# Second attention of a two-block transformer kernel: order of score matmuls, gate steps and ScalarE copies

## The chip, the cores and the metric

The program runs on one core of a Trainium2 chip. The metric is the time on the device in microseconds (us), from one launch that computes everything from the inputs in HBM to the output. TensorE (PE) multiplies, VectorE (DVE), ScalarE (ACT) and GpSimd (POOL) work on what it leaves in PSUM, and SyncE issues most loads. Each engine runs its own list of instructions in order and waits on semaphores.

## The reference

Two transformer blocks follow each other over 512 tokens of width 1024. The change is in the second one's attention. There, after an RMS norm, one wide projection `h @ w_in` gives, besides others, q, k, v (3 groups of 4 heads, head size 64) and the logits of two gates:

```
for g, (window, dil) in enumerate(((128, 1), (512, 4), (2048, 16))):
    o, lse = banded_window_attention(q_g, k_g, v_g, window // dil)   # over tokens of one residue mod dil
alpha = softmax(stack(lses))            # over the three groups
y_b = sum_g alpha_g * o_g
gates = sigmoid(gate_logits)
merged = gates[0] * (y_a @ w_branch_a) + gates[1] * (y_b @ w_branch_b)
x = x + merged @ w_out
```

The weights of the mixture over the groups make it one softmax over the keys of all three groups, and so the kernel computes it: for a head place the scores of the three groups lie side by side and get one maximum, one sum and one sum of values.

## The kernel before

Matmuls of float32 data are made of three products of rounded high and low parts. So each slab of weights (1 MB, 8 pieces of 128 rows by 256 columns) is loaded by SyncE into a ring of four buffers, its high part is copied by ScalarE (`hi`) and its low part is computed by VectorE (`lo`, or `lo_half` for half a slab) into one of the split buffers `wsq0` and `wsq1`, which the slabs use in turn. Tensor `steps(...)` is a generator: it issues six matmuls of 512 columns (two pieces of 128 rows, three products), then yields.

The second attention is done in two stages, jj = 0 and 1, one for each pair of the four head places. A stage goes so:

1. For each group g of 0, 1, 2, the slab `("qk", jj, g)` is multiplied, 8 steps: q first (m = 0), then k (m = 1), each for both heads of the pair. The result is rotated: VectorE shuffles rows and multiplies by the cosines (into `tb` for q and `X` for k), GpSimd multiplies the shuffled rows by the sines and adds, ScalarE makes the high parts (`rope_hi`, signal `a_rope`), VectorE the low parts (`rope_lo`, signal `v_rope`, tile `k2l` for k).
2. Some steps of the gate's projection. Its four slabs `("g1", n)` have 8 steps each, 32 in all, and are one generator `more` (`beside2`) that goes on through both stages, 16 steps in the first and 15 in the second; the last one comes after the loop. Every engine has its own `more`, in which each step holds what that engine has to do for it: on ScalarE step 4 of each half slab is the sigmoid of the gate, and the first step of a slab is the `hi` copy of the next slab; on VectorE step 4 is the multiplication by `row` that empties the PSUM bank, with the low parts of the next slab in steps 3 and 4 of the slab.
3. For each residue r of 0 to 3 (tokens r, r+4, ...): `scores2(jj, r)` issues the 18 score matmuls (two heads; for each of the three groups high, low and mask) into PSUM banks 2 to 4. It waits first for the rotation of group 2, and by `hold` for the exponentials of the residue before, which read the same banks. `soft2` is the maximum (VectorE) and the exponential (ScalarE), `normalise2` the division (VectorE), `turn2` the 12 transposes on TensorE (three lots of four through banks 6, 7, 6) and their three copies to `pT` on ScalarE, `values2` the product with v on TensorE, its high part on ScalarE and its low part on VectorE. Transposes follow the scores by one residue, values by two. The last two residues of stage 0 are finished inside the qk slabs of stage 1.

After the second stage `m_back` reloads a spilled tile (`M2b<-m_spill`) on ScalarE's queue; the sums of both branches and the product with `w_out` need it. The order on each engine is written out by hand in three parallel loops, one each in `tensor`, `scalar` and `vector`, and these are what the change edits. In a trace all matmuls bear line 492 and all transposes line 495, all activations line 1250, all VectorE tensor-tensor operations line 1896.

Of the kernel before, what the change touches and what calls it, by code (L numbers as in the profile page):

```python
# [8 lines left out]
P = 128  # L9
T = 512  # L10
# [21 lines left out]
M2_0, M2_1, M2_2 = 0, 516, 644  # L32
# [73 lines left out]
def emit(nc, a, out, top):  # L106
# [11 lines left out]
    S = {}  # L118
# [12 lines left out]
    ps = top.enter_context(nc.psum_tensor("ps", [P, 8 * 512], F32))  # L131
# [170 lines left out]
    mk2 = at("mk2", M_END2, BF16, sq + 31232)  # L302
    idb2 = at("idb2", 128, BF16, sq + 31624)
# [4 lines left out]
    q2v = q2[:, :].rearrange("p (g i t) -> p g i t", g=3, i=2)  # L308
    k2hv = k2h[:, :].rearrange("p (g i t) -> p g i t", g=3, i=2)
    k2lv = k2l[:, :].rearrange("p (g i t) -> p g i t", g=3, i=2)  # L310
# [162 lines left out]
        return 0 if 2 * (k + 1) <= s.nk else 1  # L473

    early_units, units = 8, 4 * 7 + 8 * 12

    def paced(it, place):

# [6 lines left out]
    def tensor(engine):  # L485
        pe = Engine(engine)
# [4 lines left out]
        def mm(o, l, r, start, stop):  # L491
            return pe.e.matmul(o, l, r, start=start, stop=stop, skip_group_check=True)  # L492
# [4 lines left out]
        def hold(b, frees):  # L497

            for signal, key in free[b]:
                pe.wait_ge(S[signal], key)  # L500
            free[b] = frees
# [285 lines left out]
        more = beside()  # L787
# [4 lines left out]
        for it in range(32):  # L792
            g, n = it // 8, it % 8
# [37 lines left out]
        for k in range(8):  # L831
            i = mm(ps[0:16, 5 * 512:5 * 512 + 1], wrv[:, k, :], sh2[:, k:k + 1], k == 0, k == 7)
# [7 lines left out]
        for r in range(2):  # L840
            for half in range(2):
                i = mm(ps[64 * half:64 * half + 64, 6 * 512 + 128 + 8 * r:6 * 512 + 136 + 8 * r], ident[:, r:P:2],
                       both[:, half:16:2], True, True)
# [48 lines left out]
        for i in range(4):  # L892
            t = tr(ps[0:16, 6 * 512 + i * P:6 * 512 + (i + 1) * P], af[:, i * 16:(i + 1) * 16], ident)
# [191 lines left out]
        turn["banks"] = [0, 1]  # L1085
        free["scores"] = free[2] + free[3] + free[4]

        def scores2(jj, r):
            for i in range(2):
                s0, s1 = (4 * 512, 3 * 512 + 256) if i else (2 * 512, 3 * 512)  # L1090
                S0 = ps[:, s0:s0 + 512]
                qa = q2v[:, 0, i, r:T:4]
                pe.wait_ge(S["a_rope"], (jj, 2, 1))
                pe.wait_ge(S["v_rope"], (jj, 2, 1))
                if i == 0:
                    hold("scores", [("a_soft", (jj, r, 1, 2))])
                mm(S0, qa, k2hv[:, 0, i, :], True, False)
                mm(S0, qa, k2lv[:, 0, i, :], False, False)
                pe.wait_ge(S["mask2_in"], "mask2")
                pe.wait_ge(S["v_set"], "idb2")  # L1100
                mm(S0, idb2[:, :], mk2[:, M2_0 + 3 - r:M2_0 + 515 - r], False, True)
                for g in (1, 2):
                    S1 = ps[:, s1 + (g - 1) * P:s1 + g * P]
                    qa = q2v[:, g, i, r:T:4]
                    mm(S1, qa, k2hv[:, g, i, r:T:4], True, False)
                    mm(S1, qa, k2lv[:, g, i, r:T:4], False, False)
                    mo = M2_1 if g == 1 else M2_2
                    t = mm(S1, idb2[:, :], mk2[:, mo:mo + P], False, True)
                t.then_inc(*S["pe_score"].tick((jj, r, i, 2)))

        def turn2(jj, r):
            for c0 in (0, 2, 4):
# [25 lines left out]
        more = beside2()  # L1138
        scored = turned = None
        for jj in range(2):  # L1140
            for g in range(3):
                pieces = steps([("qk", jj, g)], H2h, H2l, T, lambda m: [("v_rope", (jj, g, m, "cos"))])
                for _ in range(4):
                    next(pieces)
                if turned and g < 2:
                    values2(*turned)
                    turned = scored
                    scored = None
                    if turned:
                        turn2(*turned)  # L1150
                for _ in pieces:
                    pass
            for _ in range(4):
                next(more)
            for r in range(4):
                scores2(jj, r)
                next(more, None)
                next(more, None)
                if turned:
                    values2(*turned)  # L1160
                if r < 3 or jj == 0:
                    next(more, None)
                turned = scored
                scored = (jj, r)
                if turned:
                    turn2(*turned)
# [70 lines left out]
    def scalar(engine):  # L1237
# [521 lines left out]
        def turn2(jj, r):  # L1759
            for c0 in (0, 2, 4):  # L1760
                ac_.wait_ge(S["pe_turn"], (jj, r, c0, 2))
                if jj or r:
                    k = 4 * jj + r - 1
                    ac_.wait_ge(S["pe_value"], (k // 4, k % 4, 2))
                act(pT2[:, c0 * 256:c0 * 256 + 512], bank(6 + (c0 // 2) % 2), ACT.Copy).then_inc(
                    *S["a_turn"].tick((jj, r, c0, 2)))
# [11 lines left out]
        for jj in range(2):  # L1778
            for g in range(3):
                pieces = fill2(("qk", jj, g))  # L1780
                for _ in range(4):
                    next(pieces)
                if turned and g < 2:
                    values2(*turned)
                    turned = scored
                    scored = None
                    if turned:
                        turn2(*turned)
                for _ in pieces:
                    pass  # L1790
            for _ in range(4):
                next(more)
            for r in range(4):
                soft2(jj, r)
                next(more, None)
                next(more, None)
                if turned:
                    values2(*turned)
                if r < 3 or jj == 0:
                    next(more, None)  # L1800
                turned = scored
                scored = (jj, r)
                if turned:
                    turn2(*turned)
        for _ in more:
            pass
        hi(slabs["bb"])
# [82 lines left out]
    def vector(engine):  # L1890
# [783 lines left out]
        for jj in range(2):  # L2674
            for g in range(3):
                pieces = fill2(("qk", jj, g))
                for _ in range(4):
                    next(pieces)
                if turned and g < 2:
                    values2(*turned)  # L2680
                    turned = scored
                    scored = None
                for _ in pieces:
                    pass
            for _ in range(4):
                next(more)
            for r in range(4):
                soft2(jj, r)
                next(more, None)
                next(more, None)  # L2690
                normalise2(jj, r)
                if turned:
                    values2(*turned)
                if r < 3 or jj == 0:
                    next(more, None)
                turned = scored
                scored = (jj, r)
        for _ in more:
# [285 lines left out]
```

## Time and profile before

| what | value |
|---|---|
| median of 3 runs | 1957.14 us (1951.63 to 1957.41) |
| profiled execution, its own time | 1954.66 us |
| its span, first to last instruction | 1952.8 us |
| mean granted TensorE clock | 0.975 |
| PE busy | 1844.9 us, 94% of the span |
| DVE busy | 983.0 us, 50% |
| ACT busy | 654.9 us, 34% |
| POOL busy | 85.1 us, 4% |
| chain that ended last | PE 80%, DVE 9%, DMA 4%, ACT 4%, issue 2%, POOL 1% |

The span lies 1.9 us under the time of its own execution. A granted clock of 1.00 is 2.4 GHz and 0.50 is 1.2 GHz; a stretch in between is a mixture. The busy share of 94% counts matmuls that run at the lower clock in full, so it hides their slowness as well as short waits. The second attention lies between 1320 and 1516 us of the span.

### The profile page before, as it was taken

The numbers are of one execution on the slowest core, as the hardware profiler recorded it, in microseconds if no ns is written. First come the engines' busy times: TensorE is split into PE (matmuls) and PEld (weight loads), VectorE is DVE, ScalarE is ACT, GpSimd is POOL, SyncE is SP. The second block draws the span as 40 slices with busy tenths as digits, with TensorE's granted clock in tenths as the row PEclk, the third lists the DMA queues.
The fourth block names the chain that finished last, engine by engine and source line by source line (L and its number), as shares of the span: only waits on it lengthen the run. The fifth ranks groups of instructions, "written<-read, shape, count | busy, mean of one in ns | idle before, by whom it ended". The sixth has DMA issues, their size and how long they took to land.

```text
span 1952.8 us, 22760 instructions
## 1 busy us (share of the span) xinstructions
PE 1844.9 (94%) x9397; PEld 1336.6 (68%) x9403; DVE 983.0 (50%) x1620; ACT 654.9 (34%) x1126; POOL 85.1 (4%) x70
## 2 busy tenths in 40 slices
PE   5999999999999699999999899998998899999998
PEld 4877887788878434343443278897777788888886
DVE  4887887833542322231322153638384556536643
ACT  4455554432232301020110053424555333213233
POOL 0200001000000000000000000003030200000000
PEclk9999999999999699999999999999999999999999
DMA  9342423452351499999999942272121422233221
GB/s 323 127 130 77 141 76 98 130 173 87 103 231 68 167 415 421 421 422 421 420 421 422 409 141 81 70 220 65 44 84 38 156 71 85 89 119 105 73 89 43
DMA packets 174521, 355.10 MB, mean 182 GB/s; under 512 B 7154, under 2 KB 144466, under 8 KB 149074
## 3 DMA queue, kind: packets, MB, share of 16 engines
q1 hardware_dynamic: 170672, 338.85, 47.1%
q10 hardware_dynamic: 3458, 14.50, 2.1%
q8 instruction: 74, 1.21, 0.3%
q0 software_dynamic: 288, 0.30, 0.1%
q14 instruction: 29, 0.24, 0.0%
HBM read 345.53 MB, written 8.39 MB: 181 GB/s over the span
## 4 chain that ended last, share of the span: by engine, by line
PE 80%; DVE 9%; DMA 4%; ACT 4%; issue 2%; POOL 1%; SPq 0%; ACTq 0%; DVEq 0%
PE ps L492 77%; PE ps L495 3%; DMA rx<-in_w_exp_down 1%; DMA rx<-in_w_exp_up 1%; POOL X L2813 1%; DMA md<-in_w_mod 1%; DVE wsq1l L1896 1%; DVE wsp0l L1896 1%; DVE X L1905 1%; DVE small L2141 1%; ACT M L1250 1%; DVE k2l L1896 0%; ACT KR L1250 0%; DMA M2b<-m_spill 0%; DVE tb L1896 0%
## 5 line engine op out<-in xcount | busy, mean ns | idle before, releaser
L492 PE MATMUL ps<-H,wsq1h 128*128 128x512 f32 x640 | 200.4, 394 | 4.7 <-DVE wsq1l L1896 2.7
L492 PE MATMUL ps<-H,wsq0h 128*128 128x512 f32 x608 | 191.2, 396 | 0.2 <-DVE wsq0l L1896 0.2
L492 PE MATMUL ps<-rx,XE 128*64 128x512 f32 x752 | 178.5, 606 | 2.8 <-DMA rx<-in_w_exp_up 2.2
L492 PE MATMUL ps<-H,wsp1h 128*128 128x512 f32 x544 | 172.6, 399 | 1.4 <-DVE wsp1l L1896 1.4
L492 PEld LDWEIGHTS ps<-H,wsq1h 128*128 128x128 f32 x640 | 120.2, 190 | 30.6 <-issue 6.0
L492 PEld LDWEIGHTS ps<-H,wsq0h 128*128 128x128 f32 x608 | 114.5, 190 | 25.6 <-issue 2.3
L492 PE MATMUL ps<-H,wsq1l 128*128 128x512 f32 x320 | 125.3, 391 | 0.0
L492 PE MATMUL ps<-H,wsp0h 128*128 128x512 f32 x368 | 121.4, 408 | 2.1 <-ACT H L1250 2.1
L1896 DVE TENSOR_TENSOR wsq1l<-ring,wsq1h 128x1024 fp32r<-128x1024 f32 (+2 forms) x72 | 82.8, 1190 | 77.9 <-ACT wsq1h L1250 77.9
L492 PE MATMUL ps<-H,wsq0l 128*128 128x512 f32 x304 | 119.1, 392 | 0.0
L492 PEld LDWEIGHTS ps<-rx,XE 128*64 128x64 f32 x752 | 49.7, 138 | 95.9 <-issue 84.8
L492 PEld LDWEIGHTS ps<-H,wsp1h 128*128 128x128 f32 x544 | 99.8, 190 | 22.0 <-issue 3.5
L492 PE MATMUL ps<-H,wsp1l 128*128 128x512 f32 x272 | 106.8, 393 | 0.0
L1905 DVE SCALAR_TENSOR_TENSOR X<-ps,modT,X 128x512 f32<-128x512 f32 x72 | 53.8, 749 | 100.0 <-PE ps L492 100.0
L1896 DVE TENSOR_TENSOR wsq0l<-ring,wsq0h 128x1024 fp32r<-128x1024 f32 (+3 forms) x72 | 80.5, 1159 | 43.7 <-ACT wsq0h L1250 43.2
L492 PE MATMUL ps<-rx,hT 128*64 128x512 f32 x368 | 96.0, 604 | 1.5 <-DMA rx<-in_w_exp_down 1.4
L1250 ACT ACTIVATE tb<-ps 128x512 f32<-128x512 f32 (+1 forms) x44 | 26.1, 592 | 190.1 <-PE ps L492 190.1
L1250 ACT ACTIVATE wsq1h<-ring 128x1024 fp32r<-128x1024 f32 (+2 forms) x72 | 66.0, 964 | 56.0 <-PE ps L492 48.7
L492 PE MATMUL ps<-KR,wsp0h 128*128 128x512 f32 x256 | 78.8, 389 | 0.0
L1250 ACT ACTIVATE wsq0h<-ring 128x1024 fp32r<-128x1024 f32 (+3 forms) x72 | 64.2, 940 | 42.6 <-PE ps L492 40.3
L492 PEld LDWEIGHTS ps<-H,wsp0h 128*128 128x128 f32 x368 | 65.8, 192 | 16.7 <-issue 3.6
L492 PE MATMUL ps<-H,wsp0l 128*128 128x512 f32 x184 | 72.8, 396 | 0.0
(378 smaller groups left out, 3458.6 us busy)
## 6 DMA issues: line engine op xcount, KB each, us to landing
rx<-in_w_exp_gate SPq DMA_DIRECT2D x49, 1024.0 KB, 17.2
rx<-in_w_exp_down SPq DMA_DIRECT2D x46, 1024.0 KB, 20.7
rx<-in_w_exp_up SPq DMA_DIRECT2D x45, 1024.0 KB, 19.1
ring<-in_w_in SPq DMA_DIRECT2D x37, 1024.0 KB, 5.5
ring<-in_w_up SPq DMA_DIRECT2D x20, 1024.0 KB, 5.2
ring<-in_w_exp_up SPq DMA_DIRECT2D x19, 1024.0 KB, 20.5
ring<-in_w_mod SPq DMA_DIRECT2D x18, 1024.0 KB, 7.3
ring<-in_w_exp_down SPq DMA_DIRECT2D x18, 1024.0 KB, 19.0
```

The lines of the kernel that those rows point to most:

```text
L492: return pe.e.matmul(o, l, r, start=start, stop=stop, skip_group_check=True)
L495: return pe.e.transpose(o, i, idn)
L1250: return ac_.e.activation(o, i, f, **kw)
L1896: return v.e.tensor_tensor(o, x, y, op)
L1905: return v.e.scalar_tensor_tensor(o, x, s, y, op0, op1)
L2141: v.e.reduce_max(small[:, k:k + 1], ps[:, lo:lo + W + 256], axis=AX.X).then_inc(*S["v_soft"].tick((g, n, "max", i)))
L2813: return g_.e.tensor_tensor(o, x, y, op)
```

## The change

Four edits. On TensorE `scores2` gets a list of groups and waits for each group's rotation just ahead of its matmuls. The scores of groups 0 and 1 of residue 0 are issued right after the last qk slab, ahead of the gate's steps; those of group 2 follow after them. Six gate steps instead of four come ahead of group 2 (or of `soft2` on the other engines). The steps of the residues are 3, 3, 2, 2 in stage 0 and 3, 3, 2, 1 in stage 1 instead of 3, 3, 3, 3 and 3, 3, 3, 2. ScalarE takes the steps of a residue last, behind `values2` and `turn2`, where before two came ahead of `values2` and the third ahead of `turn2`.

```
--- before.py
+++ after.py
@@ -474,6 +474,11 @@
 
     early_units, units = 8, 4 * 7 + 8 * 12
 
+    def paced2(jj, r):
+
+        return {(0, 0): (2, 1), (0, 1): (2, 1), (0, 2): (1, 1), (0, 3): (1, 1),
+                (1, 0): (2, 1), (1, 1): (2, 1), (1, 2): (1, 1), (1, 3): (1, 0)}[jj, r]
+
     def paced(it, place):
 
         upto = lambda k: (units - early_units) * k // 128
@@ -1085,28 +1090,31 @@
         turn["banks"] = [0, 1]
         free["scores"] = free[2] + free[3] + free[4]
 
-        def scores2(jj, r):
+        def scores2(jj, r, groups=(0, 1, 2)):
+
             for i in range(2):
                 s0, s1 = (4 * 512, 3 * 512 + 256) if i else (2 * 512, 3 * 512)
-                S0 = ps[:, s0:s0 + 512]
-                qa = q2v[:, 0, i, r:T:4]
-                pe.wait_ge(S["a_rope"], (jj, 2, 1))
-                pe.wait_ge(S["v_rope"], (jj, 2, 1))
-                if i == 0:
-                    hold("scores", [("a_soft", (jj, r, 1, 2))])
-                mm(S0, qa, k2hv[:, 0, i, :], True, False)
-                mm(S0, qa, k2lv[:, 0, i, :], False, False)
-                pe.wait_ge(S["mask2_in"], "mask2")
-                pe.wait_ge(S["v_set"], "idb2")
-                mm(S0, idb2[:, :], mk2[:, M2_0 + 3 - r:M2_0 + 515 - r], False, True)
-                for g in (1, 2):
-                    S1 = ps[:, s1 + (g - 1) * P:s1 + g * P]
+                for g in groups:
+                    pe.wait_ge(S["a_rope"], (jj, g, 1))
+                    pe.wait_ge(S["v_rope"], (jj, g, 1))
+                    pe.wait_ge(S["mask2_in"], "mask2")
+                    pe.wait_ge(S["v_set"], "idb2")
                     qa = q2v[:, g, i, r:T:4]
-                    mm(S1, qa, k2hv[:, g, i, r:T:4], True, False)
-                    mm(S1, qa, k2lv[:, g, i, r:T:4], False, False)
-                    mo = M2_1 if g == 1 else M2_2
-                    t = mm(S1, idb2[:, :], mk2[:, mo:mo + P], False, True)
-                t.then_inc(*S["pe_score"].tick((jj, r, i, 2)))
+                    if g == 0:
+                        S0 = ps[:, s0:s0 + 512]
+                        if i == 0:
+                            hold("scores", [("a_soft", (jj, r, 1, 2))])
+                        mm(S0, qa, k2hv[:, 0, i, :], True, False)
+                        mm(S0, qa, k2lv[:, 0, i, :], False, False)
+                        mm(S0, idb2[:, :], mk2[:, M2_0 + 3 - r:M2_0 + 515 - r], False, True)
+                    else:
+                        S1 = ps[:, s1 + (g - 1) * P:s1 + g * P]
+                        mm(S1, qa, k2hv[:, g, i, r:T:4], True, False)
+                        mm(S1, qa, k2lv[:, g, i, r:T:4], False, False)
+                        mo = M2_1 if g == 1 else M2_2
+                        t = mm(S1, idb2[:, :], mk2[:, mo:mo + P], False, True)
+                if groups[-1] == 2:
+                    t.then_inc(*S["pe_score"].tick((jj, r, i, 2)))
 
         def turn2(jj, r):
             for c0 in (0, 2, 4):
@@ -1150,16 +1158,18 @@
                         turn2(*turned)
                 for _ in pieces:
                     pass
-            for _ in range(4):
+
+            scores2(jj, 0, (0, 1))
+            for _ in range(6):
                 next(more)
             for r in range(4):
-                scores2(jj, r)
-                next(more, None)
-                next(more, None)
+                scores2(jj, r, (0, 1, 2) if r else (2,))
+                for _ in range(paced2(jj, r)[0]):
+                    next(more)
                 if turned:
                     values2(*turned)
-                if r < 3 or jj == 0:
-                    next(more, None)
+                for _ in range(paced2(jj, r)[1]):
+                    next(more)
                 turned = scored
                 scored = (jj, r)
                 if turned:
@@ -1788,20 +1798,18 @@
                         turn2(*turned)
                 for _ in pieces:
                     pass
-            for _ in range(4):
+            for _ in range(6):
                 next(more)
             for r in range(4):
                 soft2(jj, r)
-                next(more, None)
-                next(more, None)
                 if turned:
                     values2(*turned)
-                if r < 3 or jj == 0:
-                    next(more, None)
                 turned = scored
                 scored = (jj, r)
                 if turned:
                     turn2(*turned)
+                for _ in range(sum(paced2(jj, r))):
+                    next(more)
         for _ in more:
             pass
         hi(slabs["bb"])
@@ -2682,17 +2690,17 @@
                     scored = None
                 for _ in pieces:
                     pass
-            for _ in range(4):
+            for _ in range(6):
                 next(more)
             for r in range(4):
                 soft2(jj, r)
-                next(more, None)
-                next(more, None)
+                for _ in range(paced2(jj, r)[0]):
+                    next(more)
                 normalise2(jj, r)
                 if turned:
                     values2(*turned)
-                if r < 3 or jj == 0:
-                    next(more, None)
+                for _ in range(paced2(jj, r)[1]):
+                    next(more)
                 turned = scored
                 scored = (jj, r)
         for _ in more:
```

## Rows read from the trace of the kernel before

**Rows 1.** What TensorE waited for from 1325 to 1530 us: total, times, longest.

```profile
PE ps L495 <- ACT pT L1250: 8.6, 8, 3.1
PE ps L492 <- ACT k2h L1250: 7.4, 2, 3.7
PE ps L492 <- DVE X L1896: 5.9, 1, 5.9
PE ps L492 <- DVE ybl L1896: 2.1, 1, 2.1
PE ps L492 <- DVE wsq1l L1896: 1.5, 1, 1.5
```

**Rows 2.** TensorE in stretches: length, busy (matmuls), granted clock, DMA share, GB/s.

```profile
1352.97:1410.69 57.72, 48.04 (x251) 0.91 0.19 55
1448.73:1508.77 60.04, 52.25 (x287) 0.89 0.17 53
1354.60:1360.40 5.80, 5.68 (x24) 1.00 0.42 120
1364.06:1368.36 4.30, 4.30 (x17) 0.67 0.16 30
1368.36:1372.81 4.45, 4.45 (x20) 0.93 0.60 210
1372.81:1376.28 3.47, 3.47 (x20) 1.00 0.00 0
1376.28:1380.49 4.21, 4.21 (x20) 1.00 0.00 0
1385.08:1389.40 4.32, 4.32 (x20) 0.61 0.00 0
1389.40:1393.94 4.54, 4.54 (x15) 0.62 0.00 0
1393.94:1398.59 4.65, 4.40 (x43) 1.00 0.71 220
1398.59:1402.26 3.67, 3.67 (x20) 1.00 0.03 11
1458.35:1463.25 4.90, 4.90 (x18) 0.50 0.31 82
1503.81:1508.77 4.96, 4.71 (x46) 1.00 0.00 0
```

**Rows 3.** TensorE in order of time: start, us, and in brackets the idle time before.

```profile
1373.89 0.44 PE L492 MATMUL ps<-k2h,q 128*128 128x128 f32 x1
...
1374.45 0.58 PE L492 MATMUL ps<-k2h,q 128*128 128x512 f32 x1
...
1410.28 0.66 PE L495 MATMUL ps<-cst,pp 128*128 128x128 f32 x4 [1.06 <-ACT pT L1250]
```

**Rows 4.** VectorE in order of time, around the first residue.

```profile
1361.17 2.79 DVE L1896 TENSOR_TENSOR k2l<-X,tbr 64x512 fp32r<-64x512 f32 x4
1363.99 2.36 DVE L1896 TENSOR_TENSOR wsq0l<-ring,wsq0h 128x1024 fp32r<-128x1024 f32 x2
1366.27 0.68 DVE L1896 TENSOR_TENSOR X<-ps,tb 128x512 f32<-128x512 f32 x1
1368.64 1.82 DVE L2643 TENSOR_REDUCE small<-ps 128x1 f32<-128x768 f32 x2 [1.69 <-PE ps L492]
```

**Rows 5.** ScalarE in order of time, exponentials of residues 0 and 1, copies behind.

```profile
1372.24 0.20 ACT L1250 ACTIVATION_READ_ACCUMULATOR pp<-ps,small 128x1 f32 x1
...
1380.31 1.28 ACT L1250 ACT_TABLE_LOAD   x1
1381.61 0.63 ACT L1250 ACTIVATE X<-X 128x512 f32<-128x512 f32 x1
1382.14 1.99 ACT L1250 ACTIVATE wsq1h<-ring 128x1024 fp32r<-128x1024 f32 x2
1384.03 1.06 ACT L1250 ACTIVATE pT<-ps 128x512 f32<-128x512 f32 x2
```

**Rows 6.** The chain of work that ended last, at the end of the second stage.

```profile
1510.35 8.02 DMA M2b<-m_spill
```

## The prediction

> **What bounds the kernel now.** The clock of the core comes first: a mean of 0.975 (in the table above), so somewhere TensorE ran below its full rate. The page's chain of work that ended last is mostly TensorE, so a microsecond counts where TensorE stands or runs slow. The change touches the second attention alone, so the next view is what TensorE waited for there [rows 1]. The reader should see four causes that the edits could touch: ScalarE's copies of transposes (8.6 us in 8 waits, longest 3.1), the rotation of group 2 (7.4 us in 2 waits of 3.7), the low part of a slab (1.5 us), and, untouched, 5.9 us for the sums behind the reload. Then the windows [rows 2]: the stage proper, from the end of the last qk slab to the end of the last transposes inside it, takes 57.72 us in the first stage. In the second, with the last gate step, a value product and one more lot of transposes, it takes 60.04. Their clocks are 0.91 and 0.89, where the stretches in them without a long wait have 1.00.
>
> The clock is the second half of the loss. The scores of one residue take 3.47 us at clock 1.00, but 4.30 at 0.67 behind the 3.7 us wait, 4.90 at 0.50 in the second stage, and 4.32 at 0.61 behind the 3.1 us wait; the two gate steps behind the latter take 4.54 at 0.62 [rows 1, 2]. Three steps at full clock take 4.21, so two take 2.81, and 1.7 us is lost there alone. Behind the 1.5 us wait the clock stayed at 1.00 [rows 1, 2]. So each wait of over 3 us costs its length and some 1.2 to 2.7 us more. A gate step is 4.21/3 = 1.40 us (three at clock 0.93 took 4.45).
>
> **The change part by part.** It removes and adds no arithmetic: the same matmuls, the same 31 steps in the loops, no DMA issue in a queue that another work would pass. What changes is when TensorE stands. I walk it.
>
> *Start of stage 0.* From 1352.97 the two first groups' scores can run: the rotation of group 1 lies one slab, some 11 us, back. Of the 3.47 us of scores, the third group's share is 2 x (1374.45 - 1373.89) = 1.12 us [rows 3], so the first two are 2.35. Behind them TensorE is at 1355.3, and the slab's low part, which it had waited for until about 1354.6, is there. Six steps at 1.40 take 8.4 us: 1363.7. The low part of k for group 2 ends at 1361.17 + 2.79 = 1363.96 [rows 4], and scores began at 1364.06 [rows 2]. This chain (VectorE, GpSimd, ScalarE, VectorE) doesn't depend on scores and stays. So both waits, 1.5 and 3.7, shrink to some 0.4 us, the clock has no reason to fall, and at 1364.06 only 1.12 us of scores are left where before 4.30 were: TensorE has them at 1365.2.
>
> *First residue's exponentials: a new wait.* VectorE makes the next slab's low parts at 1363.99 (2.36) and empties the gate's bank at 1366.27 (0.68), so it is free at 1366.95 [rows 4]: it is now late for the maximum, where before it waited for TensorE until 1368.64. From there to the end of the second exponential's sum were 1372.24 + 0.20 - 1368.64 = 3.80 us [rows 4, 5], so they end at 1370.8. TensorE has done three steps at 1365.2 + 4.2 = 1369.4 and must hold the next scores until 1370.9. The new wait is 1.5 us, as long as the one after which the clock held.
>
> *Rest of stage 0.* Residue 1: scores 3.47, three steps 4.21. Its transposes cost 1.70 us when the copies keep pace: 4.65 (values, a step, transposes) less a step of 1.4 and values of 1.5, with the usual wait of about 0.25 in them. Before they waited 3.1, as ScalarE had a table load (1.28), a sigmoid and a slab's high part (1.99) in front of the first copy at 1384.03 [rows 5]. Now that work lies between the exponentials of residues 0 and 1. From 1370.8 it is 1.28 + 0.63 + 1.99 + 1.28 (table back) = 5.2, so ScalarE is ready at 1376.0; the maximum of residue 1 is ready at 1370.9 + 3.47 + 2.15 = 1376.5. It just fits, by 0.5 us. Residues 2 and 3: scores 3.67, one step 1.4, then 4.65, which is 9.7 each [rows 2]; the 1.06 us wait of residue 3 [rows 3] shrinks to 0.25, since the sigmoid is no longer ahead of the copy. Sum: (1370.9 - 1352.97) + 3.47 + 4.21 + 1.70 + 2 x 9.7 = 46.7 us against 57.72. **11.0 us saved.**
>
> *Stage 1.* The same chain runs 94.3 us later (scores at 1458.35 for 1364.06 [rows 2]), but its last slab ended at 1448.73, which is 95.8 later: TensorE has 1.5 us less to fill. 2.35 + 8.4 brings it to 1459.5, behind the rotation: no wait. Third group and three steps, 1.12 + 4.2: 1464.8; the exponentials end at 1370.8 + 94.3 = 1465.1, a hold of 0.3. Then 3.47 + 4.21 + 1.70, residue 2 9.7. Residue 3 has only one step: scores 3.67, step 1.4, values 1.5, transposes at +6.6. The exponentials of the same residue end about 4.0 us behind the scores, then ScalarE copies the values' high part (0.4) before it takes the first transposes' copy, done at 3.67 + 4.9 = 8.6 where TensorE wants it at 7.8. Transposes thus cost 2.5: a new wait of 0.8. Sum: 16.4 + 9.4 + 9.7 + 9.1, and the tail of 4.96 as before [rows 2], is 49.6 against 60.04. **10.4 us saved.**
>
> *The tail.* The reload M2b (8.02 us [rows 6]) is issued by ScalarE behind the last copies, so it and the 5.9 us wait behind it [rows 1] move forward with them and neither grows. The qk slabs of stage 1 keep their length: their high parts are made by ScalarE one slab ahead. With the sigmoid now behind the copies, the first of these ends some 2 us later against TensorE, still 2 us before VectorE wants it.
>
> **Sum:** 11.0 + 10.4 = 21.4 us. Against the profiled execution's own time, 1954.66 - 21.4 = 1933.3. The median of the runs shown lies 2.5 us above that execution, and one run 3.0 below, so I say **1934**. If each new wait (0.4, 1.5, 0.3, 0.8) cost nothing it would be 3.0 us less, 1930, and with the spread of the runs 1927; if the holds reach 3 us, see the second case.
>
> **A rule to weigh.** The table loads on ScalarE stand in the trace with 1.28 us, and the sigmoid begins 0.02 us behind the load [rows 5]. The Trainium skill (ScalarE: Activation LUTs, What ACT_TABLE_LOAD costs) gives about 2.66 us for a switch, of which about 1.38 is a drain. By that the two switches between the exponentials of residues 0 and 1 would take 2.8 us more; the trace shows no such drain here. This bears on the third case below.
>
> **The rivals.**
> 1. *As walked* (0.70): 1934, own range 1928 to 1939.
> 2. *The hold lets the clock fall* (0.12). The scores of residue 1 must wait for residue 0's exponentials, behind VectorE's low parts. If that hold is 3 us instead of 1.5 and 0.3, it costs 1.5 and 2.7 us more and a lowered clock of 2.5 us, in both stages: 21.4 - 9.2 = 12.2 saved, 1942 by the profiled time. For it: the hold is real. Against: it needs 1.5 us that no row has.
> 3. *ScalarE becomes late for residue 1* (0.08). The margin is 0.5 us. With 2.8 us more there, the exponentials start 2.3 late and the copies, which had 0.4 us of slack, cost TensorE 1.9 us in each stage: 17.6 saved, 1937. This is what the skill's figure (ScalarE: Activation LUTs) would bring about; the rows show 1.28.
> 4. *The stage gets shorter and the end doesn't* (0.07): something behind, such as the reload or a load of `w_out`, is bound to another time, and TensorE's 5.9 us wait grows by most of the gain: 1945 to 1955. Against it: the reload's place in ScalarE's order, and a DMA share of 0.17 to 0.19 in the stages [rows 2].
> 5. *Slower* (0.03): TensorE, with more short holds of 0.25 to 1.5 us in a row, is granted the lower clock for most of both stages. Scores at 0.50 took 4.90 for 3.47, that is 1.41 times; 90 us of such work would cost 37 us more, 16 over what is saved: 1970. It decides from 21.4/0.41 = 52 us at the lower clock. Against: the stretch with value products and transposes, with its short wait, has 1.00 [rows 2].
>
> **Chances.** What differs by under 0.3% (5.9 us) can't be told from no change by a measurement of this kernel. Faster 0.92 (cases 1 to 3 and part of 4), same 0.05 (the rest of 4), slower 0.03. The range of 1927 to 1943 holds cases 1, 2 and 3.
>
> **What the profile of the changed kernel would show.** The window from the end of the last qk slab to the last transposes of the stage near 46.7 and 49.6 us, at clock 0.98 or more. The waits for the rotation under 1 us in all. Waits for `pT` of about 0.25 each, and one near 1.1 in the last residue of stage 1. A new wait of TensorE's score matmuls for ScalarE's exponentials, 1.5 and 0.3 us. The reload some 21 us earlier, its 8 us and the 5.9 us behind it unchanged. The prediction is wrong if the score matmuls of residue 0 or 2 still take over 4 us, if the hold passes 3 us, or if the 5.9 us wait grows.

## The result and the profile after

The changed kernel takes 1929.72 us (median of 4 runs, 1927.24 to 1932.09) against 1954.59 us (4 runs, 1951.63 to 1957.41): a ratio of 0.9878, 95% interval 0.9860 to 0.9897, or 20 to 27 us. The profiled execution took 1927.24 us, its span 1925.4. Line 492 is line 497 here, 495 is 500, 1250 is 1260, 1896 is 1904.

The windows of the changed kernel, TensorE alone (length, busy, matmuls, granted clock, DMA share, GB/s):

```profile
0.00:1346.27 1346.27, 1275.29 (x6745) 0.98 0.60 227
1346.27:1502.03 155.76, 143.35 (x809) 0.99 0.22 75
1502.03:1925.40 423.37, 413.74 (x1842) 0.99 0.28 90
1346.27:1393.58 47.31, 44.93 (x249) 1.00 0.22 67
1393.58:1431.50 37.92, 37.67 (x208) 1.00 0.16 56
1431.50:1481.38 49.88, 47.84 (x286) 1.00 0.19 64
1481.38:1502.03 20.65, 12.90 (x73) 0.91 0.43 153
1364.19:1367.87 3.68, 3.68 (x17) 1.00 0.02 6
```

The same cuts of the kernel before, as far as [rows 2] don't have them:

```profile
0.00:1352.97 1352.97, 1280.27 (x6745) 0.98 0.60 226
1352.97:1529.58 176.61, 150.98 (x811) 0.92 0.20 66
1529.58:1952.80 423.22, 413.67 (x1842) 0.99 0.28 90
1410.69:1448.73 38.04, 37.79 (x207) 1.00 0.16 56
1508.77:1529.58 20.81, 12.90 (x73) 0.91 0.42 152
```

The reader should see three things. First, everything the change touches lies in the second line of each: from the end of the last qk slab of stage 0 to the product with `w_out`, 176.61 us became 155.76: **20.85 us**. I call this the stretch. Second, inside it the two stages [rows 2] went from 57.72 to 47.31 and from 60.04 to 49.88, at clock 1.00 in place of 0.91 and 0.89; the qk slabs between them and the part behind them stayed to 0.2 us. TensorE's busy time in the stretch fell from 150.98 to 143.35: so 7.6 of the 20.85 us are matmuls that had run at the lower clock, and the other 13.2 are waits. Third, the two profiled executions differ by 27.4 us, and 6.7 of that lies ahead of the stretch, in code that is the same. I take that for spread between executions: over the 14 profiles of this study, all with the same code up to there, the stretch begins anywhere from 1345.01 to 1356.38 us, while what follows it lasts 423.2 to 424.5, and 23 timed runs of the kernel before lie between 1947.59 and 1958.42. So the stretch, and not a profile's whole time, prices an edit here, and 20.85 lies inside the interval of the timed runs.

What TensorE waited for in it (1325 to 1520 us):

```profile
PE ps L497 <- DVE X L1904: 5.7, 1, 5.7
PE ps L500 <- ACT pT L1260: 2.4, 8, 0.7
PE ps L497 <- DVE ybl L1904: 2.1, 1, 2.1
PE ps L497 <- ACT pp L1260: 1.9, 2, 1.2
PE ps L497 <- DVE k2l L1904: 0.4, 1, 0.4
```

L497 are the matmuls, L500 the transposes; `pT` stands for ScalarE's copies, `pp` for its exponentials, `k2l` for the rotation. Against [rows 1], the copies' 8.6 us became 2.4, the rotation's 7.4 and the slab's 1.5 became 0.4, and 1.9 us for the exponentials are new. The wait behind the reload stayed. In order of time the first two look so:

```profile
1357.44 0.46 PE L497 MATMUL ps<-k2h,q 128*128 128x128 f32 x1 [0.38 <-DVE k2l L1904]
1364.19 0.62 PE L497 MATMUL ps<-k2h,q 128*128 128x512 f32 x1 [1.25 <-ACT pp L1260]
```

And ScalarE between the exponentials of residues 0 and 1, where [rows 5] had the transposes' copies queued behind sigmoid and slab:

```profile
1363.94 0.20 ACT L1260 ACTIVATION_READ_ACCUMULATOR pp<-ps,small 128x1 f32 x1
1364.15 1.28 ACT L1260 ACT_TABLE_LOAD   x1
1365.45 0.63 ACT L1260 ACTIVATE X<-X 128x512 f32<-128x512 f32 x1
1365.98 1.99 ACT L1260 ACTIVATE wsq1h<-ring 128x1024 fp32r<-128x1024 f32 x2
1367.99 1.28 ACT L1260 ACT_TABLE_LOAD   x1
1370.02 0.90 ACT L1260 ACTIVATE pp<-ps,small 128x768 f32<-128x768 f32 x1 [0.74 <-DVE small L1910]
```

The slack of 0.5 us that was forecast is 0.74.

### The profile page after: what moved, and what is told of

The parts are those of the page before. It is cut to its first block, busy times and chain, and to the rows that moved or that the text cites. A ratio compares the mean times of both kernels' runs of the same rounds, so it can differ in the third digit from the quotient of the medians.

```text
span 1925.4 us, 22762 instructions
## 1 busy us (share of the span) xinstructions
PE 1832.4 (95%) x9395; PEld 1329.9 (69%) x9403; DVE 983.1 (51%) x1620; ACT 654.6 (34%) x1126; POOL 85.3 (4%) x70
## 4 chain that ended last, share of the span: by engine, by line
PE 80%; DVE 9%; DMA 4%; ACT 3%; issue 2%; POOL 1%; SPq 0%; ACTq 0%; DVEq 0%
PE ps L497 77%; PE ps L500 3%; DMA rx<-in_w_exp_down 1%; DMA rx<-in_w_exp_gate 1%; POOL X L2821 1%; DVE wsq1l L1904 1%; DMA md<-in_w_mod 1%; DVE k2l L1904 1%; DVE wsp0l L1904 1%; DVE X L1913 1%; DVE small L2149 1%; DVE wsq0l L1904 1%; ACT M L1260 1%; ACT KR L1260 0%; DVE tb L1904 0%
## 5 line engine op out<-in xcount | busy, mean ns | idle before, releaser
L497 PE MATMUL ps<-H,wsq1h 128*128 128x512 f32 x640 | 198.6, 392 | 3.2 <-DVE H L1913 2.0
L497 PE MATMUL ps<-H,wsq0h 128*128 128x512 f32 x608 | 189.2, 393 | 0.0
L497 PE MATMUL ps<-rx,XE 128*64 128x512 f32 x752 | 176.6, 600 | 2.8 <-DMA rx<-in_w_exp_up 2.2
L497 PE MATMUL ps<-H,wsp1h 128*128 128x512 f32 x544 | 172.8, 399 | 1.4 <-DVE wsp1l L1904 1.4
L497 PEld LDWEIGHTS ps<-H,wsq1h 128*128 128x128 f32 x640 | 119.1, 188 | 28.3 <-issue 4.1
L497 PEld LDWEIGHTS ps<-H,wsq0h 128*128 128x128 f32 x608 | 113.4, 188 | 24.5 <-issue 1.7
L497 PE MATMUL ps<-H,wsq1l 128*128 128x512 f32 x320 | 124.7, 390 | 0.0
L497 PE MATMUL ps<-H,wsp0h 128*128 128x512 f32 x368 | 119.6, 403 | 2.1 <-ACT H L1260 2.1
L497 PE MATMUL ps<-H,wsq0l 128*128 128x512 f32 x304 | 118.5, 390 | 0.0
L497 PEld LDWEIGHTS ps<-H,wsp1h 128*128 128x128 f32 x544 | 99.9, 190 | 21.9 <-issue 3.5
L497 PEld LDWEIGHTS ps<-rx,XE 128*64 128x64 f32 x752 | 49.3, 136 | 94.3 <-issue 83.2
L497 PE MATMUL ps<-H,wsp1l 128*128 128x512 f32 x272 | 106.9, 393 | 0.0
L497 PE MATMUL ps<-rx,hT 128*64 128x512 f32 x368 | 96.6, 604 | 1.4 <-DMA rx<-in_w_exp_down 1.3
L497 PE MATMUL ps<-KR,wsp0h 128*128 128x512 f32 x256 | 78.8, 389 | 0.0
L497 PEld LDWEIGHTS ps<-H,wsp0h 128*128 128x128 f32 x368 | 64.5, 188 | 16.4 <-issue 3.6
L1260 ACT ACTIVATE Yh<-ps,small 128x512 fp32r<-128x512 f32 x16 | 10.1, 684 | 184.4 <-PE ps L497 184.4
```

Of the source, the lines that this page charges most:

```text
L1260: return ac_.e.activation(o, i, f, **kw)
```

## The experiments

Stretch lengths are read as above, from a window that begins where the last qk slab of stage 0 ends and goes to the first matmul with `w_out`. All ratios are against the kernel before.

| kernel | stretch, us | less than 176.61 by | ratio, 95% interval |
|---|---|---|---|
| changed kernel | 155.76 | 20.85 | 0.9878 (0.9860 to 0.9897) |
| scores alone (e1) | 172.28 | 4.33 | 0.9973 (0.9957 to 0.9989) |
| steps alone (e2, e11) | 164.87, 164.52 | 11.74, 12.09 | 0.9946 (0.9927 to 0.9965) |
| copies first alone (e3) | 166.31 | 10.30 | 0.9954 (0.9936 to 0.9971) |
| waits filled (e4) | 169.74 | 6.87 | 0.9956 (0.9939 to 0.9972) |
| change without copies first (e5, e12) | 164.36, 164.11 | 12.25, 12.50 | 0.9949 (0.9934 to 0.9964) |
| change, later maxima (e6) | 163.73 | 12.88 | 0.9918 (0.9900 to 0.9936) |
| change, early reload (e7) | 152.49 | 24.12 | 0.9870 (0.9848 to 0.9892) |
| the same, steps shifted (e8) | 153.47 | 23.14 | 0.9871 (0.9848 to 0.9894) |
| early reload, values first (e9) | 152.09 | 24.52 | 0.9855 (0.9832 to 0.9879) |
| both (e10) | 151.25 | 25.36 | 0.9859 (0.9837 to 0.9881) |

**e1, the scores alone.** On the kernel before, `scores2` with groups as in the change, and:

```
-            for _ in range(4):
+            scores2(jj, 0, (0, 1))
+            for _ in range(4):
                 next(more)
             for r in range(4):
-                scores2(jj, r)
+                scores2(jj, r, (0, 1, 2) if r else (2,))
```

> The kernel before, with one part of the change alone: the scores of groups 0 and 1 of residue 0 right behind the last qk slab. Four gate steps ahead of group 2 and ScalarE's order as before. Theory (waits, and the lowered clock behind the long ones): TensorE has only 2.35 us of scores and four steps (5.6) to fill, so in the first stage about 3 us of waiting for the rotation remain and the clock may still fall; in the second stage about 1.6 us remain. Residue 1's scores then hang on residue 0's exponentials and start some 2 us (first stage) and 3 us (second) earlier. ScalarE's copies are as late as before. 4 to 6 us saved in all. Rival (the score order brings most of the gain): over 10 us saved.

4.33 us, as the theory had it. The waits for the rotation were 3.06 and 1.73 us; behind the first, the rest of the scores (group 2) and the steps ran at a clock of 0.75 over 6.9 us. Two groups' scores and four steps are too little work to reach the rotation.

**e2, the steps alone** (6 ahead, the new `paced2` on all engines, ScalarE's steps where they were).

> The kernel before, with the new distribution of gate steps alone (6 ahead, then 3, 3, 2, 2 and 3, 3, 2, 1) on all engines; scores in one piece, and on ScalarE the steps stay where they were, two ahead of the value copy and one ahead of the transposes' copies. Theory: the wait for the rotation falls from 3.7 to about 1 us with no lowered clock behind it, but in residue 1 ScalarE now meets a sigmoid ahead of the copies, which waits for VectorE, so the copies are late by about 3 us once more, with the lowered clock behind them. 2 to 5 us saved in all. Rival (steps alone do it): over 10 us saved, and no wait over 1 us for the copies.

11.74 us, over twice the 2 to 5 expected. Windows of e2, each the transposes of residue 0 with their wait and then the scores behind them:

```profile
1377.98:1381.99 4.01, 1.45 (x13) 1.00 0.18 40
1381.99:1385.66 3.67, 3.67 (x20) 1.00 0.69 242
1467.29:1471.29 4.00, 1.44 (x13) 1.00 0.23 65
1471.29:1474.96 3.67, 3.67 (x20) 1.00 0.62 217
```

The waits for the rotation came as expected (0.97 and 0.98 us); those for the copies were 2.56 and not 3, and the clock stayed at 1.00 behind both, where the expectation had charged for a fall. It did fall in two other places. One is behind the 0.98 us wait for the rotation in stage 1:

```profile
1450.60 0.60 PE L497 MATMUL ps<-k2h,q 128*128 128x512 f32 x1 [0.98 <-ACT k2h L1255]
...
1452.43 0.77 PE L497 MATMUL ps<-k2h,q 128*128 128x512 f32 x1
```

The scores there took 4.28 us at 0.74 and the steps 4.73 at 0.88. The other is behind the 2.05 us wait for `ybl`, in the product with `w_branch_b`. TensorE was busy for 146.38 us of the stretch, 3.0 more than in the changed kernel. Of the 11.74 us, 4.6 are less busy time (150.98 to 146.38) and 7.1 are shorter waits. So the length of a wait alone doesn't give its cost here.

**e3, copies first alone.**

```
             for r in range(4):
                 soft2(jj, r)
-                next(more, None)
-                next(more, None)
                 if turned:
                     values2(*turned)
-                if r < 3 or jj == 0:
-                    next(more, None)
                 turned = scored
                 scored = (jj, r)
                 if turned:
                     turn2(*turned)
+                for _ in range(3 if r < 3 or jj == 0 else 2):
+                    next(more)
```

> The kernel before, with ScalarE's order alone changed: value and transpose copies first, the steps of the residue behind them. Theory: both waits of 3.1 us fall to 0.25 and the lowered clock behind them goes (2.5 to 2.7 us each), the wait of 1.1 us in the first stage's last residue goes too: 11 to 12 us saved. The waits of 3.7 us for the rotation stay, with their slow scores. Rival (only the waits count, the slow matmuls have another cause): 6 to 7 us saved and the two gate steps behind the transposes still take 4.5 us.

10.30 us, under the expected 11 to 12. All eight waits for copies are at 0.25 to 0.3. The scores behind them took 3.66 us, and the two steps behind those 2.95 in place of 4.54. The lowered clock behind the rotation's waits of 3.7 us, which the edit doesn't touch, took a different time than in the kernel before. In stage 0 the three steps took 5.98 us at 0.68 in place of 4.45 [rows 2]; in stage 1 scores and steps took 0.8 less. Together that is 0.7 us of what is missing.

**e4, the waits filled.**

```
+        def filler(n):
+            for signal, key in free[5] + [("mask2_in", "mask2"), ("v_set", "idb2")]:
+                pe.wait_ge(S[signal], key)
+            for _ in range(n):
+                mm(bank(5), idb2[:, :], mk2[:, 0:512], True, True)
...
             for c0 in (0, 2, 4):
+                if c0 == 4 and r == 0:
+                    filler(11)
...
+            filler(14)
             for r in range(4):
                 scores2(jj, r)
```

> The kernel before, with no wait shortened: TensorE fills them with products that nobody reads, of the mask and the bf16 identity into the free PSUM bank 5: 14 of 512 columns (3.0 us) ahead of residue 0's scores, 11 (2.4 us) ahead of the third lot of transposes of residue 0, in both stages. Theory: what follows starts at the same time, but at the full clock: scores in 3.5 us in place of 4.3 to 4.9, two gate steps in 2.8 in place of 4.5 to 4.7: about 8 us saved by added work. Rival (the slow matmuls come from what they read or from contention with other engines, not from the idle time): no change, or some tenths slower.

Work that nobody reads made the kernel 6.87 us faster. Scores, then steps, behind each filled wait of e4:

```profile
1357.09:1360.76 3.67, 3.67 (x19) 1.00 0.08 12
1360.76:1364.98 4.22, 4.22 (x21) 1.00 0.73 242
1377.32:1380.98 3.66, 3.66 (x21) 1.00 0.02 4
1380.98:1383.93 2.95, 2.95 (x14) 1.00 0.00 0
1448.37:1452.03 3.66, 3.66 (x18) 1.00 0.07 13
1468.59:1472.26 3.67, 3.67 (x22) 1.00 0.00 0
1472.26:1475.20 2.94, 2.94 (x14) 1.00 0.00 0
```

The matmuls that count, their operands and the other engines' work are those of the kernel before; only the idle time is gone, but for 0.7 to 0.8 us of each wait. So the slow scores and steps of [rows 2] were the clock, and it fell because TensorE stood. In stage 0, 8.75 us of scores and steps became 7.89, and 8.86 became 6.61: 0.9 and 2.2 us. In stage 1, 9.68 became 7.88 and 9.01 became 6.61: 1.8 and 2.4. The stages are 3.0 and 4.1 us shorter.

**e5 and e12, the change with ScalarE's old order**, the same kernel twice.

```
                 soft2(jj, r)
+                for _ in range(paced2(jj, r)[0]):
+                    next(more)
                 if turned:
                     values2(*turned)
+                for _ in range(paced2(jj, r)[1]):
+                    next(more)
                 turned = scored
                 scored = (jj, r)
                 if turned:
                     turn2(*turned)
-                for _ in range(sum(paced2(jj, r))):
-                    next(more)
```

> The changed kernel with ScalarE's old order: in each residue the first part of the gate steps ahead of the value copy, the second part ahead of the transposes' copies. The steps alone brought 11.7 us from the end of the last qk slab to the product with w_out, with a wait of 2.6 us for the copies left in residue 0 of each stage, and 1.4 and 0.7 us in the last turned residue, and no lowered clock. Theory (the copies' order is worth only the waits it takes away once the steps are redistributed): these same waits, so 5 to 7 us slower than the changed kernel, clock 1.00 in the stages. Rival (the order is worth its wait and the lowered clock as in the kernel before, 10.3 us): slow scores behind the copies' wait, and 9 us or more slower than the changed kernel.

8.60 us slower than the changed kernel, between the theory and its rival. The waits for copies were those of e2, but for 2.12 us in place of 2.56 in stage 0, and here the clock fell behind them. Scores of e5 behind the hold of 1.25, the wait of 2.12 and the wait of 2.56 us:

```profile
1369.55:1373.85 4.30, 4.30 (x18) 0.72 0.03 10
1382.48:1386.74 4.26, 4.26 (x20) 0.69 0.49 173
1470.40:1475.04 4.64, 4.64 (x22) 0.63 0.50 174
```

The hold of 1.25 us is in the changed kernel too, in the same place, behind the same work of TensorE, and the scores behind it took 3.68 at 1.00. Two of the kernels were therefore run once more.

> The changed kernel with ScalarE's old order once more, unchanged. In the first execution the clock was 0.72 behind a hold of 1.25 us and 0.63 behind a wait of 2.56 us. Theory (a matter of the moment): the waits stay at 1.25, 2.1 to 2.6 and 2.56 us to 0.1 us, but the clock behind them may be 1.00 in one place or another. Rival (a matter of the kernel): the same places slow again, the stages as long to 0.2 us.

The same three places were slow again (0.72, 0.69, 0.63), the stretch as long to 0.3 us and the stages to 0.1, so the rival holds for this kernel.

> The steps alone once more, unchanged, for one thing: its waits of 2.56 us for the copies had the full clock behind them (3.67 us scores), where the same wait in the changed kernel with the old ScalarE order had 0.63 and scores of 4.64 us. Theory (the fall behind a wait of this length depends on when the wait comes in time, and not on the kernel): in a second execution at least one of its two waits may show slow scores. Rival (it depends on the kernel's order of work): both have 3.67 us scores again.

Here what the theory expected came. The transposes and the scores behind them in e11, to be read against e2's:

```profile
1377.54:1381.90 4.36, 1.81 (x14) 0.87 0.31 70
1381.90:1386.16 4.26, 4.26 (x21) 0.73 0.50 175
1466.76:1470.77 4.01, 1.45 (x14) 1.00 0.24 60
1470.77:1474.44 3.67, 3.67 (x22) 1.00 0.63 223
```

The same program, the same wait of 2.55 us, and once the full clock behind it, once 0.73. The 0.98 us wait in stage 1, behind which the clock fell in e2, was 1.00 us long here, with the full clock behind it. So the order of work alone doesn't decide. That the moment does is not shown: e5 and e12 fell in the same places twice. What decides it, for waits between about 1 and 2.6 us, stays open.

**e6, later maxima.** In the changed kernel VectorE takes three more maxima ahead of the real ones in residue 0, with unused results:

```
             for i in range(2):
                 n = 6 * (r % 2) + i
                 v.wait_ge(S["pe_score"], (jj, r, 1, 2))
+                for k in range(0 if r else 2 - i):
+                    o = 188 + 2 * jj + k if i == 0 else 133 + jj
+                    v.e.reduce_max(small[:, o:o + 1], ps[:, 1024:1792], axis=AX.X)
```

> The changed kernel with three more maxima over the scores on VectorE ahead of the real ones, in residue 0 of each stage, their results unused: 2.7 us more until the exponentials, so that TensorE's new hold ahead of residue 1's scores grows from 1.25 and 0.62 to about 3.9 and 3.3 us. Prices the second case of the prediction. Theory: a hold of over 3 us lets the clock fall, so each stage loses 2.7 us and some 2 to 2.7 us more in slow scores and steps: 9 to 11 us slower than the changed kernel. Rival: the clock holds, 5.4 us slower.

7.97 us slower than the changed kernel, less than the theory's 9 to 11. The holds grew to 3.68 and 3.06 us, 4.9 more in all; the rest is the clock (TensorE was busy 3.1 us longer in the stretch). Scores and three steps behind each hold of e6:

```profile
1367.14:1372.07 4.93, 4.93 (x18) 0.50 0.00 0
1372.07:1377.08 5.01, 5.01 (x21) 0.83 0.00 0
1455.47:1460.18 4.71, 4.71 (x18) 0.64 0.01 3
1460.18:1464.40 4.22, 4.22 (x20) 1.00 0.00 0
```

This prices the prediction's second case: with holds of 3.7 and 3.1 us, about 8 of the 21 us are lost.

**e7, the reload early.** Moved in the changed kernel to just behind the last exponentials, where the scores that read its place are done:

```
                 soft2(jj, r)
+                if jj and r == 3:
+                    ac_.wait_ge(S["m_out"], "m")
+                    ac_.wait_ge(S["pe_score"], (1, 3, 1, 2))
+                    load("m_back", "m", M3[:, :], m_d)
```

> The changed kernel with the reload of the spilled tile issued on ScalarE right behind the last exponentials of the second stage, when the last scores have been read, and not behind the last copies. Theory: the 8 us of the reload then lie beside the last transposes and values; the sums behind the product with w_branch_b follow that product, and TensorE's wait of 5.7 us ahead of w_out shrinks to 1 or 2 us, with no lowered clock behind it: 4 to 7 us faster than the changed kernel. Rival (the wait is set by the chain of sums on VectorE, ScalarE and GpSimd and not by the reload): less than 1 us faster.

3.27 us of the stretch, a little under the theory's 4 to 7; the timed medians, 1929.50 and 1929.72, don't show it. The wait ahead of `w_out` fell from 5.7 to 2.5:

```profile
PE ps L497 <- DVE X L1905: 2.5, 1, 2.5
PE ps L497 <- DVE ybl L1905: 2.1, 1, 2.1
```

The theory had no lowered clock behind this wait. That missed: the 3.5 us behind it ran at 0.51, close to the 0.53 behind the 5.7 us wait of the changed kernel.

**e8, e9 and e10.** e8 is e7 with steps 4, 2, 2, 2 and 3, 2, 2, 2. e9 is e7, and e10 is e8, with the last residue's values ahead of the slab's split on ScalarE and VectorE:

```
         turn2(*scored)
-        hi(slabs["wo2", 0])
         values2(*scored)
+        hi(slabs["wo2", 0])
...
         values2(*turned)
-        lo(slabs["wo2", 0])
         values2(*scored)
+        lo(slabs["wo2", 0])
```

> As the early reload, and the steps shifted: 4, 2, 2, 2 in stage 0 (in place of 3, 3, 2, 2) and 3, 2, 2, 2 in stage 1 (in place of 3, 3, 2, 1). Theory: the hold of 1.25 us ahead of residue 1's scores goes, but its transposes come 1.4 us earlier against the exponentials and wait about 0.6 us more for ScalarE's copies; in stage 1 the copies' wait of residue 3 falls from 0.66 to 0.25 and about as much comes back in residue 1. Up to 1 us faster than the early reload alone. Rival: the sigmoid of step 12 delays the copies or the exponentials, and it is 1 us or more slower.

> As the early reload, and the last residue's values (high part on ScalarE, low part on VectorE) taken ahead of the split of the first w_out slab, on both engines. Theory: TensorE's wait of 2.05 us for the low part inside the product with w_branch_b shrinks to under 1 us, and since that product now ends only some 2.5 us ahead of the sums, half of this or more reaches the product with w_out: 1 to 2 us off the 152.5 us from the end of the last qk slab to the product with w_out. Rival: the sums on VectorE set the start of w_out and move by nothing. In the whole time the difference to the changed kernel (4 to 5 us) is about as large as the spread of the runs.

> The same with the shifted steps (4, 2, 2, 2 and 3, 2, 2, 2). Theory: the shifted steps are worth 1 us in stage 0 and nothing in stage 1, so it is up to 1 us shorter than the one before in the stages; what was lost behind them was the clock, which fell in that run behind the 2.05 us wait and should not with the shorter wait. About 150 us from the end of the last qk slab to the product with w_out. Rival: the longer stretch behind the stages came from the steps and stays.

e8's stage 0 took 46.33 us against the changed kernel's 47.31 (e7 has 47.29), its stage 1 49.96 against 49.88. But behind the 2.05 us wait for `ybl` the clock fell in e8 (0.65 over 4.88 us) and not in e7, and e8's stretch came out 1.0 longer where up to 1 less was expected. The clock fell behind this wait in e1, e2 and e11 too (0.52 to 0.68 over 3.5 us). There the wait for `w_out`, still set by the late reload, became shorter, and wait and product together grew by no more than 0.6 us; in e8 they grew by 1.9. In e9 the wait for `ybl` is gone, and the wait ahead of `w_out` grew from 2.5 to 4.0 us: the stretch is 0.4 us shorter in place of 1 to 2, so the rival was nearly right: the sums set the start of `w_out`. e10 has the shortest stretch, 151.25 us, 0.84 less than e9, with the shifted steps worth 1.0 us in stage 0 and no lowered clock behind the stages, as its theory had it. Its ratio is 0.9859. By the timed runs it can't be told from the changed kernel (the intervals overlap), only by the stretch, 4.5 us.

## Why the prediction was right, step by step

- *Start of stage 0.* Forecast: both waits shrink to 0.4 us and the last scores begin with the rotation's end. Measured 0.38. The rotation's chain didn't move: the low part of k still ended about 11.0 us behind the last qk slab.
- *The new hold.* Forecast 1.5 and 0.3 us, measured 1.25 and 0.62. It was found by following VectorE's order and not TensorE's, as the maximum had become late for VectorE's own work. The sums over both stages agree to 0.1 us. That the hold left the clock alone was partly luck. The prediction argued from one wait of 1.5 us behind which the clock held; behind the same 1.25 us hold it was 1.00 in the changed kernel, e7 and e9, and 0.72 in e5 and e12.
- *Copies.* Forecast 0.25 each and an extra 0.8 us in the last residue; measured 0.25 and 0.66 there, so 0.4 extra. ScalarE's margin of 0.5 us was 0.74. The table loads took 1.28 us, and the sigmoid began 0.02 us behind its load. The third case did not arise. The Trainium skill (ScalarE: Activation LUTs, What ACT_TABLE_LOAD costs) gives about 1.28 us for the load and 1.38 for a drain, 2.66 in all for a switch. By that page, as an estimate, two switches would have made the exponentials some 2 us late; the trace agrees on the load and shows no drain.
- *Stages.* 46.7 and 49.6 forecast, 47.31 and 49.88 measured. The 0.9 us too few are mostly two prices: the scores of residue 1, behind the hold, took 3.68 to 3.70 us where the sum had 3.47, and the step between scores and values took 1.57 where it had 1.40. The new wait in stage 1's last residue, 0.4 shorter than forecast, went the other way.
- *The tail.* Forecast: the reload moves along and the 5.9 us wait doesn't grow. It took 7.86 us and the wait was 5.7. The fourth case fell; e7 shows that this wait was in fact the reload, for 3.3 us of it.
- *Clock.* That it falls behind the waits of over 3 us was read from the rows, and e4 shows it. Over all kernels it fell behind each wait of 3.06 us or more in the stages, and behind some of 0.98 to 2.56, which the prediction took for harmless up to 1.5. A fall was priced a little high: 1.2 to 2.7 us beside the wait, where e4 gives 0.9 to 2.4, since the sum took 3.47 us for scores that take 3.66 right behind a wait even at full clock. The fifth case, a low clock through many short holds, did not come: 1.00 in both stages.
- *The median* is 1929.7 for 1934 predicted. 21.4 us were forecast and the stretch gave 20.85; with that, the median of 1954.59 would give 1933.7. No window ties the 4 us between this and 1929.7 to the change: they lie inside the interval of the timed runs, and the part ahead of the stretch varies by 11 us from one profile to another.

What each part is worth depends on the others. Alone they give 4.3, 11.7 and 10.3 us, 26.4 together, and in one kernel 20.85. The overlap, as far as the windows tell, is the copies' wait and the lowered clock behind it: both the new steps (which put ScalarE's slab copy between two exponentials) and the new ScalarE order shorten that wait. Scores and steps together (e5) are worth hardly more than the steps alone, 12.3 against 11.7 to 12.1. TensorE was busy for 146.4 us of the stretch in both, so both lost 3.0 us to the clock, in different places. The early scores took away 3.1 us of waits for the rotation and the slab but brought 1.9 us of holds, and of the rest 1.4 came back as a longer wait for `w_out` (6.0 for 4.6 us). With the copies' order on top they reach 20.85. Steps and copies together without the early scores were not run, so what the early scores add to the whole change is not shown.

## What to carry to other kernels

Price a wait of TensorE with what runs behind it, and compare its busy time in the same stretch, which grows by what the lower clock costs: here a wait of 3.1 us cost up to 5.5 (in stage 1, scores and two steps of 9.0 us that e4 made 6.6), and the windows by granted clock show it where busy shares hide it. When work is moved ahead to fill a wait, look for the engine that becomes late next by reading its own order (here VectorE's low parts ahead of the maximum). And price an edit by a stretch between two fixed points of the program when its gain is of the size of the spread between executions.

## What the hardware showed that was not expected

- A wait of 2.56 us was followed by the full clock twice in e2, but in e11, the same program, once by 0.73 and once by 1.00. A wait of 1.25 us was followed by 1.00 in the changed kernel and by 0.72 in e5 and e12. A wait of 0.98 us was followed by 0.74 in e2, one of 1.00 in the same place by 1.00 in e11. In the stages it fell behind every wait of 3.06 us and more. What decides in between was not settled.
- How long it stays low differs too: behind a wait of 3.7 us, scores and three steps took 8.75 us in the kernel before and 4.31 + 5.98 = 10.3 us in e3.
- 25 matmuls a stage without any use made the kernel faster by 6.87 us (e4).
